# Causal mask of the forget attention: from TensorE products into a second copy of the gate sums

## What is computed

```python
log_f = jax.nn.log_sigmoid(f_logit + b_f)
c = jnp.cumsum(log_f, axis=1)                     # the gate sums, one row of 512 a head
s = jnp.einsum('bhqd,bhkd->bhqk', qi, k) * scale  # a block of 128 queries
s = s + ci[..., None] - c[:, :, None, :]
mask = key_pos[None, :] <= qpos[:, None]
s = jnp.where(mask[None, None], s, NEG)           # NEG = -1e30
p = jax.nn.softmax(s, axis=-1)
out = jnp.einsum('bhqk,bhkd->bhqd', p, v)
```

## Time and profile before

| | us |
|---|---|
| median of 3 runs | 1642.12 |
| lowest and highest | 1641.85, 1642.72 |
| the profiled execution | 1642.05 |
| its span, first to last instruction | 1640.2 |

### The profile page before, as it was taken

The page is one execution under the profiler, slowest core; times in us unless marked ns, Lnnn a source line. Parts: engine busy times, 40 slices in busy tenths (PEclk is TensorE's granted clock), DMA queues, the critical chain, the costliest instruction groups (busy, mean ns, idle before and its releaser), DMA issues.

```text
span 1640.2 us, 19997 instructions
## 1 busy us (share of the span) xinstructions
PE 1620.8 (99%) x8264; PEld 1331.3 (81%) x8264; DVE 817.5 (50%) x1224; ACT 655.7 (40%) x983; POOL 517.7 (32%) x253
## 2 busy tenths in 40 slices
PE   9999999999999999999999999999999999999997
PEld 6888888788878888888887767789878788888886
DVE  7787766665655365444443647681356621111113
ACT  7533333333333333554445463424435642332321
POOL 1000000000044434334334334353323465555541
PEclk9999999999999999999999999999999999999998
DMA  6454434333345323233323241122112233232321
GB/s 238 151 195 131 147 103 136 108 129 122 122 148 188 124 74 116 91 103 103 103 90 117 81 154 64 52 85 73 39 52 68 75 115 102 91 103 90 103 78 52
DMA packets 52674, 177.05 MB, mean 108 GB/s; under 512 B 6364, under 2 KB 7004, under 8 KB 52200
## 3 DMA queue, kind: packets, MB, share of 16 engines
q1 hardware_dynamic: 52584, 175.78, 32.3%
HBM read 170.49 MB, written 2.12 MB: 105 GB/s over the span
## 4 chain that ended last, share of the span: by engine, by line
PE 90%; DVE 5%; ACT 2%; issue 1%; DMA 0%; SPq 0%; DVEq 0%; POOL 0%; ACTq 0%; POOLq 0%
PE banks L411 89%; PE banks L414 2%; DVE ACC L1130 1%; DVE wl L1094 1%; DVE X L1078 1%; DVE ada L1078 1%; ACT wh L1905 1%; ACT T L1902 0%; DMA maskf<-cst_dram 0%; DVE HL L1078 0%; ACT Sc L1902 0%; ACT L1902 0%; DVE ML L1078 0%; ACT HH L1902 0%; DVE mx L1165 0%
## 5 line engine op out<-in xcount | busy, mean ns | idle before, releaser
L2452 POOL TENSOR_TENSOR wl<-raw,wh 128x1024 fp32r<-128x1024 f32 x172 | 426.1, 2482 | 541.8 <-ACT wh L1905 541.8
L411 PE MATMUL banks<-HH,wh 128*128 128x512 f32 x1040 | 413.6, 398 | 1.3 <-ACT T L1902 1.0
L411 PE MATMUL banks<-HL,wh 128*128 128x512 f32 x1040 | 402.6, 390 | 0.0
L1905 ACT ACTIVATE wh<-raw 128x1024 fp32r<-128x1024 f32 x246 | 257.9, 1054 | 313.4 <-PE banks L411 306.2
L411 PE MATMUL banks<-HH,wl 128*128 128x512 f32 x1040 | 285.8, 390 | 0.0
L411 PEld LDWEIGHTS banks<-HH,wh 128*128 128x128 f32 x1040 | 195.4, 188 | 48.0 <-issue 4.6
L411 PEld LDWEIGHTS banks<-HL,wh 128*128 128x128 f32 x1040 | 195.4, 188 | 41.4 <-issue 1.4
L411 PEld LDWEIGHTS banks<-HH,wl 128*128 128x128 f32 x1040 | 194.9, 188 | 41.8 <-issue 1.0
L2461 POOL TENSOR_TENSOR OL<-T,OH 128x512 fp32r<-128x512 f32 x21 | 28.2, 1343 | 452.8 <-ACT OH L1905 452.8
L411 PE MATMUL banks<-wh,HH 128*128 128x256 f32 x448 | 129.0, 288 | 0.0
L411 PE MATMUL banks<-wl,HH 128*128 128x256 f32 x448 | 126.7, 283 | 0.0
(11 more groups left out here) (341 smaller groups left out, 2497.2 us busy)
## 6 DMA issues: line engine op xcount, KB each, us to landing
raw<-wst_dram SPq DMA_DIRECT2D x294, 512.0 KB, 3.3
CB<-sums_dram SPq DMA_DIRECT2D x12, 256.0 KB, 3.1
D<-dec_dram SPq DMA_DIRECT2D x12, 256.0 KB, 2.9
X<-xT_dram SPq DMA_DIRECT2D x4, 512.0 KB, 6.3
out_dram<-X SPq DMA_DIRECT2D x8, 256.0 KB
QS<-QX SPq DMA_DIRECT2D x24, 64.0 KB, 2.7
KSw<-KX SPq DMA_DIRECT2D x24, 64.0 KB, 2.0
MX<-memT_dram SPq DMA_DIRECT2D x2, 512.0 KB, 9.1
```

What stands on the lines that cost most here:

```text
L411: return pe.eng.matmul(dst, w, x, start=start, stop=stop, skip_group_check=True)
L1905: return eng.activation(dst, src, ACT.Copy)
L2452: tt(wl[:, q, :], raw[:, i % NRAW, :], wh[:, q, :].bitcast(F32), ALU.subtract).then_inc(*by_pool("low", u))
```

## The change

The mask is added once a head, by GpSimd, to a second copy `CM` of the gate sums, and the diagonal block of each shift on VectorE reads `CM` in place of `CB`. In detail:

- TensorE: the 48 mask products and their weight loads are gone. The f32 product of each block is now the last of its group and sets the mark.
- VectorE: a shift of block 3, 2 or 1 is split into the part left of the diagonal (reads `CB`) and the diagonal 128 columns (reads `CM`), the latter behind a new wait for "masked"; block 0 has the diagonal part alone. 48 shifts become 84. One of two casts at the start is gone, the other makes an f32 mask `mask`.
- GpSimd: twelve adds of 128x512, `CM = CB + mask` (the mask repeated four times), each behind the landing of that head's `CB` and the last shift of the head before (head 0: behind "sums kept", since `CM` lies where `CT` lay).
- SyncE: the load of `CB` for head h also waits for the add of head h - 1.

```diff
-    identb = at("identb", [128, 128], 165, BF16)
-    maskb = at("maskb", [128, 128], 165.25, BF16)
+    mask = at("mask", [128, 128], 165)
...
+    CM = at("CM", [128, T], C0 + 28)
...
                 pe.wait_ge(*free[b])
-                mm(o, Qt[:, j, 128 * i:128 * i + 128], Kt[:, j, 0:n], i != 0, False)
-                pe.wait_ge(done("masks"))
-                mm(o[:, 128 * i:n], identb[:, :], maskb[:, :], False, True).then_inc(*by_pe("f scored", h, i))
+                mm(o, Qt[:, j, 128 * i:128 * i + 128], Kt[:, j, 0:n], i != 0, i != 2).then_inc(*by_pe("f scored", h, i))
...
-        eng.tensor_copy(identb[:, :], ident[:, :]).then_inc(*by_dve())
-        eng.tensor_copy(maskb[:, :], maskf[:, :]).then_inc(*by_dve("masks"))
+        eng.tensor_copy(mask[:, :], maskf[:, :]).then_inc(*by_dve("masks"))
...
-                stt(s, bank[b][:, OFF_Q[i]:OFF_Q[i] + n], cq[:, i, h:h + 1], CB[:, 0:n], ALU.add,
+                o = OFF_Q[i]
+                if i:
+                    stt(s[:, 0:n - 128], bank[b][:, o:o + n - 128], cq[:, i, h:h + 1], CB[:, 0:n - 128], ALU.add,
+                        ALU.add).then_inc(*by_dve())
+                dve.wait_ge(done("masked", h))
+                stt(s[:, n - 128:n], bank[b][:, o + n - 128:o + n], cq[:, i, h:h + 1], CM[:, n - 128:n], ALU.add,
                     ALU.add).then_inc(*by_dve("f shifted", h, i))
...
+        def mask_sums(h):
+
+            pool.wait_ge(done("cb", h), done("masks"), done("f shifted", h - 1, 1) if h else done("sums kept"))
+            tt(CM[:, :].rearrange("p (i m) -> p i m", i=4), CB[:, :].rearrange("p (i m) -> p i m", i=4),
+               mask[:, :].rearrange("p (i m) -> p i m", i=1).to_broadcast([128, 4, 128]), ALU.add).then_inc(*by_pool("masked", h))
+
+        mask_sums(0)
         for p in range(6):
             units(2)
             finish(0, 2 * p - 1 if p else 15)
+            mask_sums(2 * p + 1)
             units(2)
             finish(0, 2 * p)
+            if p < 5:
+                mask_sums(2 * p + 2)
...
-                sp.wait_ge(done("sums kept"), done("f shifted", h - 1, 1) if h else done("gates summed"))
+                sp.wait_ge(done("sums kept"), done("f shifted", h - 1, 1) if h else done("gates summed"),
+                           done("masked", h - 1) if h else None)
```

## The result

| | before, us | after, us |
|---|---|---|
| median (10 runs each) | 1642.56 | 1637.81 |
| lowest and highest | 1641.41, 1643.20 | 1637.12, 1638.84 |
| span of the profiled execution | 1640.2 | 1635.6 |

The ratio is 0.9973, with a 95% interval from 0.9965 to 0.9980: 4.75 us faster, 0.3%. The forecast was 1636.9 (5.2 us less) in a range of 1635.8 to 1639.5.

The account below looks back on a forecast made before the run. From 150 to 470 us TensorE's own stream, busy 320.00 of 320.00 us, was taken as the bound. 8 x 0.45 + 4 x 0.40 = 5.2 us off, other engines free: 1636.9 us, range 1635.8 to 1639.5.

Parts of the forecast that it names:

- TensorE's share: Scores of all twelve heads: dropping 48 mask products takes 5.2 us off TensorE, bounds 2.6 to 10.6 us.
- The terms of 0.45 and 0.40 us a head: TensorE's saving per head: 0.45 us for eight heads followed by a unit, 0.40 for four followed by transposes.
- The argument from the attend products: Attend has the same four f32 widths without masks: 2.39 us to the next unit's second product, against 2.84 for scores.
- the rival with the slots alone: On TensorE only the masks' own start distances go, f32 products behind still start late: 2.6 us less, 1639.5; chance 0.09.
- the split into slot and late start: Each mask's 0.11 us on TensorE: about 0.06 its own start distance, about 0.05 the f32 product behind lacking its weights.
- The gain is kept behind the stage: After about 470 us TensorE arrives 5.2 us early everywhere, and the whole gain was expected to stay.
- VectorE's additions: Three of four shifts per head split, 36 more instructions: 0.65 to 0.75 us a head, 7.4 us listed in twelve.
- Head 11: Tightest place for normalised scores before TensorE's transposes: 1.9 us to spare, 0.8 us after the change.
- So VectorE's additions cost nothing: VectorE's extra work stays inside its listed covers; only at the last head would any excess over 0.8 us cost, once.
- GpSimd's adds: Twelve 128x512 adds of about 1.3 us, 16 us on an engine idle 305 of 320 us; price nothing.
- The second rival: VectorE late at the last head, or a wait behind the stage, gives part back: 1638.1 to 1639.3 us; chance 0.11.
- the slower rival: Adds hold up VectorE's weight work behind each head; decides from 4.7 us an add, at worst 1679.6 us; chance 0.03.

Follow-up runs that it names:

- no masks: The kernel before with its 48 mask products left out and nothing put in their place; median 1637.21 us beside 1641.92 before, ratio 0.9969.
- split shifts only: The changed kernel without GpSimd's twelve adds and their waits, diagonal parts reading CB; median 1637.12 us beside 1641.92 before, ratio 0.9971.
- late adds: The changed kernel with adds for even heads from 2 on held until VectorE has kept that pair's keys; medians 1637.56 and, again, 1637.11 us.
- the two runs on the masks: The kernel before with each head's four mask products issued first (1640.51 us, ratio 0.9988), or every mask product issued twice (1644.81 us, ratio 1.0015).

## Why the prediction was right, and where it was off

- **TensorE's share**, forecast 5.2 us from the distance between starts, measured 5.10 in the stage (no masks, split shifts only, late adds: 324.38 in all three). The terms of 0.45 and 0.40 us a head are 0.44 and 0.39. The argument from the attend products, which have the same four widths, held, and the rival with the slots alone (2.6 us) is out; the split into slot and late start, then only argued, is now shown by the two runs on the masks, its reason isn't.
- **"The gain is kept behind the stage"**: from the end of the stage to the last instruction it is 1158.4 us before and 1158.7 after, less than what differs from one execution to another.
- **VectorE's additions**, forecast 0.65 to 0.75 us a head: the listed durations add up to the 0.62 of the forms, but the way to the keys grew by 0.38 only, since the two parts of a split shift have no wait between them and overlap (384 and 128 columns take 0.88 us together and not 0.95). Busy time says the same: from 150 to 480 us VectorE has 219.87 us with the split shifts only and 215.34 with no masks, 4.5 more and not 7.4. So the 7.1 us of the changed kernel's page met the forecast by luck: about 4.5 of split shifts and, which nobody had forecast, about 3 of instructions held by the adds. The error was to the safe side. Head 5's scalings leave 3.6 us to the transposes where they left 4.4.
- **Head 11**, forecast 0.8 us left of 1.9: 1.1 us. It was not the tight place:

```profile
465.55 1.27 DVE L1305 TENSOR_SCALAR Sc<-Sc,rs 128x512 f32<-128x512 f32 x4
...
467.94 1.26 PE L414 MATMUL banks<-ident,Sc 128*128 128x128 f32 x10
```

- **"So VectorE's additions cost nothing" is the step that failed**, by 0.7 us. The list of who waits behind VectorE had the scores, the exponents and the low halves of the weights, and left out that VectorE also empties TensorE's banks: the keys of pair 1 stand behind two adaptive sums and two low halves, with 1.23 us of cover in the kernel before, less than any place that I listed. I had looked at the low halves in the earlier trace rows, which stand directly ahead of these keys, and stopped there.
- **GpSimd's adds**, forecast 1.3 us each at no price: 3.03 us in the mean. Groups by form, the changed kernel (busy us, mean ns, idle before):

```profile
L2488 POOL TENSOR_TENSOR CM<-CB,mask 128x512 f32<-128x512 f32 x12 | 36.4, 3032 | 159.7 <-DMA CB<-sums_dram 159.7
```

  In itself that cost nothing, since CM was still early each time, by 12.7 us or more. Four of the adds lasted over 4 us, which the prediction had named as a sign of being wrong; in these it was GpSimd that waited. The hold that it puts on VectorE cost half of the pause at head 1. The second rival had this mechanism ("VectorE can be held by GpSimd") but looked for it at head 11; the slower rival had it behind each head, and of the places where VectorE was held only head 1 had too little cover. That there is only one pause was not foreseen either: the keys of pair 3, behind head 5, had 1.36 us of cover before and 0.56 in the changed kernel, less than a hold of 1.0 us. Behind that head GpSimd was the one that waited, in all the runs whose adds lie there.
- The predicted 1636.9 is 0.9 us below the measured 1637.81. Of that 0.44 lies in the start: the forecast took off from a median of 1642.12, and the kernel before has 1642.56 over ten runs. The gain itself is 4.75 us for 5.2. In the stage it is 4.42, short by 0.1 of TensorE's share and 0.7 of the pause; the 0.3 us between 4.42 and 4.75 is within what medians of this kernel do.

## What to carry to other kernels

Price a small product on a full TensorE by the starts around it, and find in the same stage a set of products of the same widths without it; its listed duration (10.6 us here) said twice what it was worth. Before extra work on another engine is called hidden, list everything that engine does for the full one, the emptying of banks too, and take the least cover along its queue; then take off what the full engine itself will gain, since that gain eats the same cover. Work on GpSimd that runs beside VectorE can be moved by one condition to a moment when nobody waits for VectorE.

## What the runs showed of the hardware

In these traces a GpSimd add of two inputs in SBUF and VectorE's instructions of two inputs in SBUF don't run side by side. Alone an add of 128x512 lasted 1.28 to 1.30 us. At head 4, in the changed kernel, it lasted 4.32 us, while VectorE went through an adaptive sum and two low halves without a break:

```profile
273.69 1.28 DVE L1076 SCALAR_TENSOR_TENSOR ada<-raw,sc,ada 128x1024 f32<-128x1024 f32 x1
274.88 2.35 DVE L1092 TENSOR_TENSOR wl<-raw,wh 128x1024 fp32r<-128x1024 f32 x2
...
274.06 4.32 POOL L2488 TENSOR_TENSOR CM<-CB,mask 128x512 f32<-128x512 f32 x1 [5.74 <-DMA CB<-sums_dram]
```

VectorE's end is 277.23, the add's 278.38, 1.15 us later: GpSimd waited for almost all of it, and VectorE for none. At head 1 it was the other way round: the add came in between two adaptive sums, and the second lasted 2.31 us. VectorE was held like this for 0.4 us or more beside four of the twelve adds (behind the scores of heads 0, 1, 3 and 7: one instruction each, of 2.32, 2.31, 1.71 and 1.71 us), and GpSimd beside ten of them (1.9 to 4.3 us). Each time the held instruction of VectorE ended 1.08 us after the add. That fits with each waiting for what the other has begun.

What lets the add in is in part visible. Behind heads 3 and 7 an instruction that reads PSUM (`mod<-banks`) stands between two low halves, and the second low half is the one held:

```profile
246.90 0.68 DVE L1112 TENSOR_REDUCE mod<-banks 128x4 f32<-128x512 f32 x1
247.50 1.71 DVE L1092 TENSOR_TENSOR wl<-raw,wh 128x1024 fp32r<-128x1024 f32 x1
```

The same holds with the adds moved late, where a copy from PSUM stands ahead of the held sum. At heads 0 and 1 the add came in between two adaptive sums with nothing between them, while it never came in between a sum and a low half or between two low halves with nothing between them; why, no run here decides.
